# Two-layer streaming encoder on eight cores: lanes half a layer apart from the first weights on, each with its own f32 loads in the first pass

## The chip, the cores and the metric

The kernel runs on all eight cores of one Trainium2 chip. Each core computes one prompt stream and one sample stream; the cores exchange nothing and read the same weights. The metric is the device time of the slowest core, in microseconds.

## What is computed

A network of two layers, for 4096 new frames ("prompt") and 16 frames ("sample") per core, width 1024. Every layer is a mixer and a gated feed-forward block (FFN), each behind an rmsnorm:

```python
for layer in range(DEPTH):            # DEPTH = 2
    # even layer: conv_mixers; odd layer: attention || spatial gating
    x = x + mixer(rmsnorm(x))
    x = x + swiglu(rmsnorm(x, norm_ffn[layer]), w_gate_up[layer], w_down[layer])

def swiglu(h, w_gate_up, w_down):     # FFN_HIDDEN = 2816
    g, up = jnp.split(h @ w_gate_up, 2, axis=-1)
    return (jax.nn.silu(g) * up) @ w_down
```

The even mixer has an input projection of 1024 x 2560, a causal depthwise convolution of width 31 with a layernorm, a convolution of width 3, and an output projection of 1024 x 1024. The odd mixer has an input projection of the same size, attention over the last 576 keys with a relative bias, a spatial gating in blocks of 128 frames, and an output projection. All weights come as f32 and are used as bf16.

## The kernel before

**Tiles and slots.** The prompt's 4096 frames are 8 tiles of 512. All weights of both layers are cut into 96 pieces, called slots (`NPS`, line 458): per layer 10 of the input projection, 4 of the output projection, 22 of gate and up, 12 of down. A slot is 128 x 8 x 256 elements, 512 KB as bf16; 8 of the 12 down slots of a layer have 7 parts instead of 8 (448 KB). For one tile a slot is 16 matmuls of 128x512 (`ws`, line 558), for the sample 16 matmuls of 128x16. Weights don't stay on the core: each tile runs through all 96 slots again. The slots pass through `ring`, nine buffers in SBUF (line 330); buffers 7 and 8 are scratch of the sample until it is done.

**Two lanes and the sample.** Lane A (`lanes[0]`) does tiles 0, 2, 4, 6, lane B (`lanes[1]`) tiles 1, 3, 5, 7, and the sample S goes once through the 96 slots. Each is a generator that yields segments. While the program is built, the loop at lines 1275 to 1325 picks the next segment by a model of time with durations written into it, so the order on every engine is fixed when the program is built. `rank` (lines 1302 to 1311) decides between segments that the model has ready within 0.15 us of each other. Between the lanes, B goes first if A is at least a number of slots ahead, else A: `LAG0` = 3 slots while B is in its first tile, `LAG` = 24 behind it. When the favoured lane isn't ready the other goes.

**Weights in the first pass.** In its first pass a slot is loaded once, from the f32 input `w`, by a DMA on POOL's queue that casts to bf16 (`load_next`, line 465). Both lanes and the sample use that one buffer, which is free again after the third use (`consume`, line 488; the 3 stands in line 493). As lane A comes to a slot, `touch` (line 477) has SP's queue write the bf16 buffer to `wsc` in HBM; the first four slots (`SKIP`) are not written. From each lane's second tile on every lane has buffers and loads of its own, from `wsc`, or from `w` for the first four slots. The DMAs of POOL and of SP each go out in order: a reload that waits holds up all behind it on its queue. A reload waits for TensorE's last use of the buffer and, where the buffer was stored, for that store.

**Other traffic.** x comes in four pieces of 512 KB per tile and y leaves in four, between the down slots of layer 1. The width-31 convolution needs 16 shifted copies of its input per tile (`U<-U`, line 747). The table of attention biases (`Tb`, loaded through `Vb<-rbt`, 1536 KB) is made in the first pass by the prologue, from the flag "late" on, which lane B sets at its fifth gate-up pair (line 644); layer 1 of every lane waits for the flag "Tb" (line 845).

In the views, `L440` is every matmul, `L445` every DMA, `L398` every ScalarE activation, `L411`, `L415` and `L421` VectorE's work; `hT`, `U`, `cat` are a lane's activations, `SM` and parts of `ring` the sample's.

Of the kernel before, what the change touches and what calls it, by code (L numbers as in the profile page):

```python
# [22 lines left out]
LAG = 24  # L23
LAG0 = 3
# [22 lines left out]
class Sched:  # L47
# [176 lines left out]
    def dma(self, eng, fn, sem, rd, wr, us, issue=0.07, load=False):  # L224
# [30 lines left out]
        if load:  # L255
            s = max(start + issue, self.load_free)
            self.load_free = s + us
            b["end"] = max(b["end"], s + us + 2.0)
        else:
            b["end"] = max(b["end"], start + issue + 2.0 + us)  # L260
# [34 lines left out]
def build_program(n_tiles=NPT):  # L295
# [22 lines left out]
    with ExitStack() as es:  # L318
# [146 lines left out]
        def load_next(L):  # L465
            while len(L.loaded) < NPS * L.n_tiles and L.bufs:
                g = len(L.loaded)
                nk = slot_k[g % NPS]
                first = g < NPS or g % NPS < SKIP
                s = L.bufs.pop(0)  # L470
                src = (wv if first else wsv)[g % NPS][:, 0:nk, :]
                dma("pool", ring[:, s, 0:nk, :], src, "ring%d" % s, us=(3.5 if first else 1.8) * nk / 8, load=True)
                L.loaded.append(s)
                if g == NPS - 1:
                    lanes[1].loaded = list(L.loaded)

        def touch(L, sl):
            g = L.th.pos
            if g == len(stored) and g < NPS:
                nk = slot_k[g]  # L480
                if g >= SKIP:
                    dma("sp", wsv[g][:, 0:nk, :], ring[:, sl, 0:nk, :], "st%d" % sl, us=1.8 * nk / 8, load=True)
                stored.append(g)

        def owner(th):
            return lanes[1 if th is thB and th.pos >= NPS else 0]

        def consume(L):
# [4 lines left out]
            if users[O.i, g] == (3 if g < NPS else 1):  # L493
                s = O.loaded[g]
                if s in (4, 5, 6, 8) and len(lanes[0].loaded) >= NPS:
                    O = lanes[1]
                O.bufs.append(s)
# [770 lines left out]
        lanes[0].bufs, lanes[1].bufs = [0, 1, 2], []  # L1268
        load_next(lanes[0])
        first_x(lanes[1], 1, "pool")  # L1270
        lanes[0].bufs.extend([3, 4, 5, 6])
        load_next(lanes[0])
        for th in (thA, thB):
            th.step(None)
        while threads:
            cand = []
            for th in threads:
# [28 lines left out]
                elif th is thS:  # L1306
                    rank = 2 if th.pos <= min(thA.pos, thB.pos + 1) else 4
                elif thA.done or thB.done:
                    rank = 3
                else:  # L1310
                    rank = 3 if (thA.pos - thB.pos >= (LAG0 if thB.pos < NPS else LAG)) == (th is thB) else 5
# [7 lines left out]
            if th is thS and th.done:  # L1319
                lanes[0].bufs.append(7)  # L1320
                load_next(lanes[0])
                O = lanes[1 if len(lanes[0].loaded) >= NPS else 0]
                O.bufs.append(8)
                load_next(O)
# [150 lines left out]
```

How the kernel before makes its waits and increments, by code:

```python
            def emit(handle, eng):  # L1351
                seen = {}
                n = 0
                for fn, waits, sig, inc in S.ops[eng]:
                    for ch, val in waits:
                        v = rank_of[ch][val] if ch in rank_of else S.batches[ch][val]["n"]
                        if seen.get(ch, 0) >= v:
                            continue
                        handle.wait_ge(sems[ch], v)
                        seen[ch] = v
                    ins = fn(handle)
                    if sig in rank_of:
                        n += 1
                        if n in rank_of[sig]:
                            ins.then_inc(sems[sig], 1)
                    elif sig is not None:
                        ins.then_inc(sems[sig], inc)
```

## Time and profile before

| what | us |
|---|---|
| median of 3 runs | 3000.2 (2998.64 to 3558.65) |
| profiled execution, device time | 3000.1 |
| its span, slowest of 8 cores | 2998.5 (the cores lie between 2985.4 and 2998.5) |
| TensorE busy in the span | 2933.1 |

"Busy" is the time in which an engine works on an instruction. The DMA share is the mean busy share of the core's 16 DMA engines, and PEclk is the clock that TensorE was granted, as a part of full speed. A DMA's landing time runs from its issue to its completion and so contains what it queues behind; a queue's share of the 16 engines is what its packets took.

### The profile page before, as it was taken

Reading aid. Unit: us, or ns where it says so; the run is one execution under the profiler, and the core shown is the slowest. Engines: PE = TensorE matmul, PEld = TensorE weight load, DVE = VectorE, ACT = ScalarE, POOL = GpSimd, SP = SyncE. Lnnn points to the kernel's source line nnn. Section 1 sums busy time; section 2 is a strip of 40 time slices with the busy share of each in tenths; the row PEclk is TensorE's granted clock in tenths of the full one; section 3 lists DMA queues with packets and bytes.
Section 4 is the critical chain, followed back from the end, with each engine's and each line's share of the span. In section 5 each row is a group of like instructions: output and inputs, shape, how many; then the busy total and the mean of one; then the engine's idle time right before and its main releaser. Section 6 shows DMA issues by size and latency. Waiting matters only on the chain.

```text
span 2998.5 us, 43471 instructions; the slowest of 8 cores (2985.4 to 2998.5 us)
## 1 busy us (share of the span) xinstructions
PE 2933.1 (98%) x17072; PEld 1388.0 (46%) x17072; DVE 1108.3 (37%) x1452; ACT 1017.2 (34%) x1140; POOL 386.1 (13%) x801
## 2 busy tenths in 40 slices
PE   7999999999999999999999999999999999999999
PEld 3444455444444445444444445444444444544444
DVE  5632144411253224534333333453334242444321
ACT  4421145311133225463232224455223221536410
POOL 1000000000011111111111111111111111111111
PEclk9999999999999999999999999999999999999999
DMA  9766653376983444335566544334665654434434
GB/s 192 159 153 149 140 111 102 85 166 139 217 205 113 149 153 136 118 133 164 167 172 190 174 149 147 127 127 138 172 191 163 178 154 154 134 126 155 141 127 153
DMA packets 125223, 451.83 MB, mean 151 GB/s; under 512 B 17953, under 2 KB 20513, under 8 KB 124898
## 3 DMA queue, kind: packets, MB, share of 16 engines
q0 software_dynamic: 92256, 348.17, 43.4%
q1 hardware_dynamic: 32770, 100.89, 10.8%
q8 instruction: 141, 2.31, 0.3%
q14 instruction: 56, 0.46, 0.1%
HBM read 427.93 MB, written 66.36 MB: 165 GB/s over the span
## 4 chain that ended last, share of the span: by engine, by line
PE 92%; DMA 4%; DVE 2%; ACT 1%; SPq 1%; issue 1%; POOL 0%; DVEq 0%; ACTq 0%; POOLq 0%
PE ps L440 92%; DMA xT<-xp 2%; DMA U<-U 1%; SPq L445 1%; ACT U L398 1%; DVE U L411 0%; DMA ring<-wsc 0%; DVE U L421 0%; ACT hT L398 0%; DVE hT L415 0%; DVE rs L411 0%; ACT cat L398 0%; ACT rs L398 0%; DVE ps L411 0%; ACT L398 0%
## 5 line engine op out<-in xcount | busy, mean ns | idle before, releaser
L440 PE MATMUL ps<-hT,ring 128*128 128x512 bf16 x7680 | 1707.2, 381 | 16.3 <-DVE hT L415 6.4
L440 PEld LDWEIGHTS ps<-hT,ring 128*128 128x128 bf16 x7680 | 743.5, 98 | 928.2 <-issue 63.3
L398 ACT ACTIVATE U<-ps 128x1024 f32<-128x1024 f32 (+3 forms) x448 | 434.0, 981 | 1130.6 <-PE ps L440 924.5
L440 PE MATMUL ps<-U,ring 128*128 128x512 bf16 x3328 | 748.9, 379 | 0.0
L411 DVE TENSOR_TENSOR U<-ps,U 128x1024 bf16<-128x1024 f32 (+2 forms) x240 | 276.4, 1152 | 1012.6 <-PE ps L440 894.8
L440 PEld LDWEIGHTS ps<-U,ring 128*128 128x128 bf16 x3328 | 319.7, 98 | 386.8 <-issue 11.7
L445 POOL DMA_DIRECT2D ring<-wsc x552 | 294.7, 534 | 1568.2 <-PE ps L440 1524.5
L398 ACT ACT_TABLE_LOAD x164 | 210.4, 1283 | 291.1 <-PE ps L440 248.2
L398 ACT ACTIVATE hT<-xT 128x1024 f32<-128x1024 f32 (+1 forms) x118 | 124.1, 1055 | 354.1 <-DVE xT L411 174.6
L411 DVE TENSOR_TENSOR xT<-ps,xT 128x1024 f32<-128x1024 f32 x96 | 117.2, 1223 | 275.8 <-PE ps L440 275.8
L415 DVE SCALAR_TENSOR_TENSOR hT<-rs,vecT,xT 128x512 bf16<-128x512 f32 x256 | 172.3, 746 | 47.3 <-ACT rs L398 44.8
L445 POOL DMA_DIRECT2D ring<-w x120 | 63.7, 533 | 743.5 <-PE ps L440 722.6
L411 DVE TENSOR_TENSOR ps<-ps,Tb 128x768 f32<-128x768 f32 (+1 forms) x144 | 97.8, 695 | 72.7 <-PE ps L440 70.2
L440 PE MATMUL ps<-cat,ring 128*128 128x512 bf16 x512 | 121.0, 379 | 0.7 <-DVE SM L411 0.7
L440 PE MATMUL ps<-ring,hT 128*128 128x256 bf16 x1024 | 119.7, 276 | 1.4 <-ACT cat L398 1.4
L440 PEld LDWEIGHTS ps<-ring,hT 128*128 128x128 bf16 x1024 | 99.8, 99 | 20.2 <-issue 5.6
L411 DVE TENSOR_TENSOR U<-ps,xT 128x1024 f32<-128x1024 f32 x32 | 39.2, 1224 | 141.1 <-PE ps L440 141.1
L421 DVE TENSOR_SCALAR U<-ps,vecT 128x1024 f32<-128x1024 f32 x32 | 41.1, 1284 | 100.2 <-ACT U L398 97.8
L440 PEld LDWEIGHTS ps<-cat,ring 128*128 128x128 bf16 x512 | 49.2, 98 | 59.2 <-issue 1.5
L440 PE MATMUL ps<-U,ones 128*64 128x512 bf16 (+1 forms) x480 | 64.0, 303 | 4.7 <-ACT U L398 4.6
L440 PE MATMUL ps<-U,convW 128*32 128x512 bf16 x1024 | 58.5, 387 | 6.1 <-DMA U<-U 5.9
L440 PE MATMUL ps<-U,Vb 128*64 128x512 bf16 (+1 forms) x480 | 62.8, 299 | 0.0
(141 smaller groups left out, 1097.2 us busy)
## 6 DMA issues: line engine op xcount, KB each, us to landing
ring<-wsc POOLq DMA_DIRECT2D x456, 512.0 KB, 3.7
ring<-w POOLq DMA_DIRECT2D x104, 512.0 KB, 7.2
ring<-wsc POOLq DMA_DIRECT2D x96, 448.0 KB, 3.6
wsc<-ring SPq DMA_DIRECT2D x76, 512.0 KB, 5.0
U<-U SPq DMA_DIRECT2D x128, 134.5 KB, 8.0
yp<-U SPq DMA_DIRECT2D x32, 512.0 KB, 5.9
xT<-xp SPq DMA_DIRECT2D x22, 512.0 KB, 8.1
ring<-w POOLq DMA_DIRECT2D x16, 448.0 KB, 5.8
```

Source lines behind the costliest of these rows:

```text
L398: return e.activation(out=out, in_=in_, func=func, **kw)
L411: return S.add("dve", lambda e: e.tensor_tensor(out=out, in0=in0, in1=in1, op=op), [in0, in1], [out], dcost(in0))
L415: return S.add("dve", lambda e: e.scalar_tensor_tensor(out=out, in0=in0, scalar=scalar, in1=in1, op0=op0, op1=op1), rd, [out], dcost(in0, 1))
L421: return e.tensor_scalar(out=out, in0=in0, scalar1=s1, scalar2=None, op0=op0)
L440: return S.add("pe", lambda e: e.matmul(out, lhsT, rhs, start=start, stop=stop), [lhsT, rhs], [out], c)
L445: return S.dma(eng, lambda e: e.dma_start(out=out, in_=in_), sem, [in_], [out], us, issue, load)
```

## The change

Each lane now has its own buffers and loads from the first slot on: A (with the sample) buffers 0 to 3, B buffers 4 to 6; after the sample A gets 7 and B gets 8. In the first pass each lane loads every slot from f32. A buffer of lane A is free after two uses in the first pass (A and S), one of B after one. The lag of 3 holds only until B has done two slots; from then on it is 30 slots, where a layer has 48. The bf16 copies are written while lane A is in its second pass, whose loads are therefore from f32 too; lane B's second pass and all later ones load copies. All 96 slots are now stored. The costs in the model of time change as well: an f32 load counts 3.4 us instead of 3.5, and a store occupies the modelled DMA without waiting for earlier loads.

In the program this makes 288 loads from `w` (240 of 512 KB, 48 of 448 KB) where there were 120 (104 and 16), 480 loads from `wsc` (400 and 80) where there were 552 (456 and 96), and 96 stores where there were 92.

```diff
--- before.py
+++ after.py
@@ -20,7 +20,7 @@
 NEG = -30000.0
 SLOT = 4096
 KB = 12
-LAG = 24
+LAG = 30
 LAG0 = 3
 JIT = 4
 SKIP = 4
@@ -252,7 +252,10 @@
                 snap[a] = v
         b["snap"] = snap
         self.t[eng] = start + issue
-        if load:
+        if load == "store":
+            self.load_free = max(start + issue, self.load_free) + us
+            b["end"] = max(b["end"], start + issue + 2.0 + 2 * us)
+        elif load:
             s = max(start + issue, self.load_free)
             self.load_free = s + us
             b["end"] = max(b["end"], s + us + 2.0)
@@ -465,36 +468,31 @@
         def load_next(L):
             while len(L.loaded) < NPS * L.n_tiles and L.bufs:
                 g = len(L.loaded)
-                nk = slot_k[g % NPS]
-                first = g < NPS or g % NPS < SKIP
+                n = g % NPS
+                nk = slot_k[n]
+                first = g < NPS or n >= len(stored)
                 s = L.bufs.pop(0)
-                src = (wv if first else wsv)[g % NPS][:, 0:nk, :]
-                dma("pool", ring[:, s, 0:nk, :], src, "ring%d" % s, us=(3.5 if first else 1.8) * nk / 8, load=True)
+                dma("pool", ring[:, s, 0:nk, :], (wv if first else wsv)[n][:, 0:nk, :], "ring%d" % s, us=(3.4 if first else 1.8) * nk / 8,
+                    load=True)
                 L.loaded.append(s)
-                if g == NPS - 1:
-                    lanes[1].loaded = list(L.loaded)
 
         def touch(L, sl):
             g = L.th.pos
-            if g == len(stored) and g < NPS:
-                nk = slot_k[g]
-                if g >= SKIP:
-                    dma("sp", wsv[g][:, 0:nk, :], ring[:, sl, 0:nk, :], "st%d" % sl, us=1.8 * nk / 8, load=True)
+            if L.i == 0 and NPS <= g < 2 * NPS and g - NPS == len(stored):
+                nk = slot_k[g - NPS]
+                dma("sp", wsv[g - NPS][:, 0:nk, :], ring[:, sl, 0:nk, :], "st%d" % sl, us=1.8 * nk / 8, load="store")
                 stored.append(g)
 
         def owner(th):
-            return lanes[1 if th is thB and th.pos >= NPS else 0]
+            return lanes[1 if th is thB else 0]
 
         def consume(L):
             g = L.th.pos
             O = owner(L.th)
             L.th.pos += 1
             users[O.i, g] = users.get((O.i, g), 0) + 1
-            if users[O.i, g] == (3 if g < NPS else 1):
-                s = O.loaded[g]
-                if s in (4, 5, 6, 8) and len(lanes[0].loaded) >= NPS:
-                    O = lanes[1]
-                O.bufs.append(s)
+            if users[O.i, g] == (2 if O.i == 0 and g < NPS else 1):
+                O.bufs.append(O.loaded[g])
                 load_next(O)
 
         flags = set()
@@ -1265,11 +1263,10 @@
         dma("sp", smp.cst, sst[:, :], "sst", us=4)
         thP.step(None)
         S.add("pool", lambda e: e.memset(tailA[:, 0, 0:1], 0.0), [lanes[0].xT[:, 0:2, :]], [tailA[:, 0, 0:1]], 0.1)
-        lanes[0].bufs, lanes[1].bufs = [0, 1, 2], []
+        lanes[0].bufs, lanes[1].bufs = [0, 1, 2, 3], [4, 5, 6]
         load_next(lanes[0])
         first_x(lanes[1], 1, "pool")
-        lanes[0].bufs.extend([3, 4, 5, 6])
-        load_next(lanes[0])
+        load_next(lanes[1])
         for th in (thA, thB):
             th.step(None)
         while threads:
@@ -1304,11 +1301,11 @@
                 elif not seg.slot:
                     rank = 1
                 elif th is thS:
-                    rank = 2 if th.pos <= min(thA.pos, thB.pos + 1) else 4
+                    rank = 2 if th.pos <= thA.pos else 4
                 elif thA.done or thB.done:
                     rank = 3
                 else:
-                    rank = 3 if (thA.pos - thB.pos >= (LAG0 if thB.pos < NPS else LAG)) == (th is thB) else 5
+                    rank = 3 if (thA.pos - thB.pos >= (LAG0 if thB.pos < 2 else LAG)) == (th is thB) else 5
                 cand.append((t, rank, th, b))
             t0 = min(c[0] for c in cand)
             t, rank, th, b = min((c for c in cand if c[0] <= t0 + 0.15), key=lambda c: c[1])
@@ -1317,11 +1314,9 @@
                 pairs_free.remove(b)
             th.step((b, owner(th).loaded[th.pos] if seg.slot else None))
             if th is thS and th.done:
-                lanes[0].bufs.append(7)
-                load_next(lanes[0])
-                O = lanes[1 if len(lanes[0].loaded) >= NPS else 0]
-                O.bufs.append(8)
-                load_next(O)
+                for i in range(2):
+                    lanes[i].bufs.append(7 + i)
+                    load_next(lanes[i])
             threads[:] = [x for x in threads if not x.done]
 
         fin = []
```

**TensorE in the first FFN of the first tiles.** In the rows `hT0` is lane A's input, `hT1` lane B's, `SM` the sample's; x16 is one slot of a lane. Before:

```order
L440 MATMUL ps<-hT1,ring 128x512 x16
L440 MATMUL ps<-SM,ring 128x16 x16
L440 MATMUL ps<-hT0,ring 128x512 x16
L440 MATMUL ps<-hT1,ring 128x512 x16
L440 MATMUL ps<-SM,ring 128x16 x16
```

Changed, from lane B's eighth slot and the slots 14 to 17 of lane A on:

```order
L443 MATMUL ps<-hT1,ring 128x512 x16
L443 MATMUL ps<-SM,ring 128x16 x32
L443 MATMUL ps<-hT0,ring 128x512 x32
L443 MATMUL ps<-SM,ring 128x16 x16
L443 MATMUL ps<-hT0,ring 128x512 x16
L443 MATMUL ps<-SM,ring 128x16 x16
L443 MATMUL ps<-hT0,ring 128x512 x16
```

Before, lane A and lane B take turns slot by slot. Changed, after lane B's eighth slot (first row) lane A and the sample go on alone, up to lane A's slot 37.

**TensorE ahead of lane A's first attention layer, changed.** `rs0` and `hT0` with `o1024` are lane A's norm, `kT 128x512` belongs to the making of the bias table, and the last row is lane A's slot 48:

```order
L443 MATMUL ps<-hT1,ring 128x512 x32
L443 MATMUL ps<-rs0,o1024 128x512 x2
L443 MATMUL ps<-hT0,o1024 128x512 x2
L443 MATMUL ps<-hT1,ring 128x512 x48
L443 MATMUL ps<-kT 128x512 x2
L443 MATMUL ps<-hT1,ring 128x512 x96
L443 MATMUL ps<-SM,ring 128x16 x16
L443 MATMUL ps<-hT0,ring 128x512 x16
```

Eleven slots of lane B (18 to 28) stand in a row here (x32, x48 and x96), with four more (14 to 17) a little ahead of them. Lane A is 30 slots ahead when they begin and 19 when its layer 1 does.

**TensorE from lane A's second tile on.** `convW` is the convolution of width 31. Before, from lane A's first slots to the convolution of lane B:

```order
L440 MATMUL ps<-hT0,ring 128x512 x32
L440 MATMUL ps<-rs1,o1024 128x512 x2
L440 MATMUL ps<-hT1,o1024 128x512 x2
L440 MATMUL ps<-hT0,ring 128x512 x128
L440 MATMUL ps<-hT1,ring 128x512 x16
L440 MATMUL ps<-U0,convW 32x512 x128
L440 MATMUL ps<-hT1,ring 128x512 x48
L440 MATMUL ps<-U0,o512 128x512 x2
L440 MATMUL ps<-rs0,o512 128x512 x2
L440 MATMUL ps<-hT1,ring 128x512 x96
L440 MATMUL ps<-cat0,ring 128x512 x8
L440 MATMUL ps<-U0,ring 128x512 x8
L440 MATMUL ps<-U1,convW 32x512 x128
```

Changed, lane A's first slots and what follows them:

```order
L443 MATMUL ps<-hT0,ring 128x512 x32
L443 MATMUL ps<-hT1,ring 128x512 x64
L443 MATMUL ps<-hT0,ring 128x512 x16
L443 MATMUL ps<-hT1,ring 128x512 x48
L443 MATMUL ps<-U0,convW 32x512 x128
L443 MATMUL ps<-hT1,ring 128x512 x48
L443 MATMUL ps<-U0,o512 128x512 x2
L443 MATMUL ps<-rs0,o512 128x512 x2
L443 MATMUL ps<-hT0,ring 128x512 x16
L443 MATMUL ps<-hT1,ring 128x512 x16
```

Before, both lanes do their ten input slots together, and the two convolutions stand 9 slots apart. Changed, lane A's convolution stands among lane B's output projection and gate and up slots of layer 1 (x64, x48, x48).

**SP's queue, where the stores stand.** Before, from the start of the program:

```order
L445 DMA ring<-sst 128x252
L445 DMA U0<-U0 32x2152 x16
L445 DMA wsc<-ring 128x2048 x2
L445 DMA U1<-U1 32x2152 x16
L445 DMA wsc<-ring 128x2048 x4
L445 DMA cas<-ring 512x1x30
L445 DMA cbs<-ring 512x1x2
L445 DMA wsc<-ring 128x2048 x14
```

Changed, from the end of lane A's first tile on:

```order
L448 DMA xT0<-xp 128x1024
L448 DMA yp<-U0 128x1024
L448 DMA xT0<-xp 128x1024
L448 DMA ys<-SM 128x128
L448 DMA yp<-U0 128x1024
L448 DMA wsc<-ring 128x2048 x4
L448 DMA U0<-U0 32x2152 x16
L448 DMA wsc<-ring 128x2048 x13
L448 DMA hT1<-xp 128x1024
L448 DMA wsc<-ring 128x2048 x3
L448 DMA yp<-U1 128x1024
```

The stores moved from the first weights on to behind the first tile's last y piece, where lane A's replicas and lane B's x and y pieces go out as well.

## Rows read from the trace of the kernel before

**Rows 1.** The page: busy us of each engine (part 1), POOL's DMA queue (part 3)

```profile
PE 2933.1 (98%) x17072; PEld 1388.0 (46%) x17072; DVE 1108.3 (37%) x1452; ACT 1017.2 (34%) x1140; POOL 386.1 (13%) x801
...
q0 software_dynamic: 92256, 348.17, 43.4%
```

**Rows 2.** Windows: engines' busy us by stretch, then granted clock, DMA share, GB/s

```profile
0.00:150.00 150.00, 128.08 (x1018) 60.86 (x1019) 86.45 (x168) 67.50 (x102) 13.14 (x30) 0.98 0.83 176
150.00:375.00 225.00, 225.00 (x1409) 107.20 (x1408) 58.93 (x78) 38.84 (x49) 17.44 (x35) 1.00 0.66 148
375.00:600.00 225.00, 215.87 (x1708) 116.08 (x1707) 99.12 (x159) 106.44 (x151) 15.25 (x38) 0.98 0.46 99
600.00:750.00 150.00, 150.00 (x947) 71.86 (x946) 25.46 (x29) 21.05 (x27) 11.62 (x22) 1.00 0.71 153
750.00:975.00 225.00, 210.63 (x1252) 94.87 (x1251) 88.90 (x119) 60.33 (x70) 25.37 (x48) 0.97 0.72 179
975.00:2998.50 2023.50, 2003.54 (x10745) 937.17 (x10742) 749.42 (x899) 723.06 (x742) 303.25 (x628) 1.00 0.49 152
```

**Rows 3.** Timeline of TensorE, 17 to 70: start, us, line, operands, count

```profile
17.63 1.09 PE L440 MATMUL ps<-SM,ring 128*128 128x16 bf16 x16 [2.15 <-DMA ring<-w]
...
44.80 0.55 PE L440 MATMUL ps<-SM,ring 128*128 128x16 bf16 x16
...
45.41 17.43 PE L440 MATMUL ps<-hT,ring 128*128 128x512 bf16 x80
62.87 7.10 PE L440 MATMUL ps<-U,convW 128*32 128x512 bf16 x128
```

**Rows 4.** DMA, 150 to 375: queues (packets, MB, share), issues (count, KB, landing)

```profile
q0 software_dynamic: 4392, 15.44, 45.2%
q1 hardware_dynamic: 4898, 17.57, 20.7%
...
wsc<-ring SPq DMA_DIRECT2D x23, 512.0 KB, 3.8
ring<-w POOLq DMA_DIRECT2D x23, 512.0 KB, 7.0
ring<-w POOLq DMA_DIRECT2D x8, 448.0 KB, 5.4
wsc<-ring SPq DMA_DIRECT2D x8, 448.0 KB, 2.5
```

**Rows 5.** DMA, 30 to 40, with no other queue at work

```profile
q0 software_dynamic: 479, 1.75, 102.5%
```

**Rows 6.** DMA, 1000 to 1100

```profile
q0 software_dynamic: 3729, 14.90, 45.5%
...
ring<-wsc POOLq DMA_DIRECT2D x22, 512.0 KB, 3.5
ring<-wsc POOLq DMA_DIRECT2D x8, 448.0 KB, 3.3
```

**Rows 7.** DMA, 40 to 150

```profile
q1 hardware_dynamic: 4608, 11.82, 41.7%
...
wsc<-ring SPq DMA_DIRECT2D x14, 512.0 KB, 10.1
...
U<-U SPq DMA_DIRECT2D x32, 134.5 KB, 6.8
```

**Rows 8.** DMA, 750 to 850

```profile
q0 software_dynamic: 2809, 10.01, 58.0%
q1 hardware_dynamic: 3656, 12.04, 41.1%
...
ring<-w POOLq DMA_DIRECT2D x9, 512.0 KB, 11.7
...
wsc<-ring SPq DMA_DIRECT2D x2, 512.0 KB, 20.9
```

**Rows 9.** Waits of POOL: us in total, times, longest

```profile
POOL ring L445 <- DMA wsc<-ring: 23.0, 3, 10.7
```

## The prediction

> **What bounds the kernel now.** I read the page's busy line first, then busy time by stretch, then who is waited for, then the DMA queues. TensorE is busy 2933.1 of 2998.5 us [rows 1]; all that a change of order can touch is the 65.4 us in which it idles, plus what a lowered clock costs. The stretches say where they lie [rows 2]: 21.9 us in the first 150, none in 150 to 375, 9.1 in 375 to 600 (both lanes at attention together), none in 600 to 750, 14.4 in 750 to 975 (the lanes are pulled apart from 3 slots to 24 while all 16 DMA engines are full), 20.0 in the 2023.5 us of steady state and tail behind it. The clock column reads 0.98, 0.98 and 0.97 in the three stretches with stalls and 1.00 elsewhere: about 0.02 x 128 + 0.02 x 216 + 0.03 x 211 = 13 us. So faster by 2% (60 us, about what a measurement of this kernel can tell from no change) would need nearly all of the idle time and clock loss at once.
>
> The other resource is DMA. In the first pass a slot's weights are loaded once for both lanes and the sample, so a load is wanted about every 7 us and the DMA share is only 0.66 [rows 2]. Prices per full slot (512 KB as bf16): TensorE needs (62.87 - 45.41) / 5 = 3.49 us for a lane's 16 matmuls and 0.41 us (45.21 - 44.80) for the sample's [rows 3]. For DMA I divide a queue's share by its transfers. 150 to 375: 45.2% of 225 us = 101.7 us over 23 + 8 x 0.875 = 30 loads from f32 = 3.4 us of all 16 engines each, with a store beside each; on SP's queue 20.7% of 225 = 46.6 us, less 4.8 for a table of 1536 KB, over 30 stores: 1.4 to 1.45 us [rows 4]. Alone on the engines such loads are cheaper: in 30 to 40 us POOL's queue moved 1.75 MB, 3.34 slots, in 102.5% of 10 us: 3.07, say 3.0 to 3.1 us [rows 5]. The bf16 copies in steady state: 45.5 us over 29 loads = 1.57 us [rows 6]. Conv replicas: SP's queue spent 41.7% of 110 = 45.9 us in 40 to 150; less 14 stores at 1.45, 25.6 us for 32 issues, so 0.80 each, 12.8 us for a tile's 16 [rows 7]. An x or y transfer moves the bytes of a copy's load, 512 KB: 1.6 us.
>
> **The change, part by part.** Traffic: weights are loaded from f32 288 times instead of 120 and from the bf16 copies 480 times instead of 552; stores are 96 instead of 92. In full slots: 164 more at 3.4, 70 fewer at 1.57, 4 more at 1.45: 558 - 110 + 6 = 454 us of DMA, so POOL's queue, 43.4% now [rows 1], should read about 58%, or down to 56% as far as loads without stores beside them are cheaper. Whether that costs time is a question of stretches. I walk the new order by slots (A, B the lanes, S the sample; "A14" is lane A's 15th weight slot) and set TensorE's need against DMA's, first at the dearer 3.4 us.
>
> A0-13 with B0-7: TensorE 22 x 3.49 + 14 x 0.41 + 14.2 for one lane's conv (2 x 7.10 [rows 3]) + 2 = 99 us; DMA 22 x 3.4 + 12.8 + 6.4 for the second x = 94. A14-37 with S alone: 94 against 82. A38-47 with B8-28: 123 against 120 (a conv, a set of replicas and the table in it). A48-61, B29-34 and the sample's attention: about 100 against 71. A62-95 with B35-57: 221 against 195. In each of these DMA keeps up, and without stores, at 3.1 us, it has a tenth to spare. The stretch that does not fit is A96-129 with B58-95. Lane A now loads its second pass from f32 too, and the stores fall there. TensorE: 71 full slots x 3.49 + 14.2 + 6 = 268 us. DMA: 67 loads from f32 (34 for A, 33 for B), four bf16 loads 6, 34 stores x 1.45 = 49, ten x and y transfers 16, replicas 13. A store stands beside every second load, so I price these between the two rows, at 3.2: 214, in all 298 us, short by 30. Slack of earlier stretches is lost, because only nine buffers can hold loads ahead; full at the start and nearly empty at the end they give back about six loads, 19 us. So I take **+10 us** there. Bounds: 0 at 3.1 us, where the shortage of 22 about fits the buffers (and in 750 to 850 the two queues took 58.0 + 41.1 = 99% of the engines [rows 8], inside a stretch that idles 14.4 us in all); +43 at 3.4 with no help from the buffers, +23 with it. Behind it a pair of slots needs 3.4 + 1.45 + 1.57 = 6.4 us of DMA against 6.98, so the backlog melts by 0.6 us a pair while lane B's replicas come: **+3** (0 to +12).
>
> The start: the first load still lands at about 17 us [rows 3], but four loads of lane A now stand ahead of lane B's x and three of B's behind it, and A4's load, issued when A0 is done near 24 us, stands behind all of it (7 loads x 3.1 + 6.4 = 28 us from 9 us on, then its own 3.1: about 40). TensorE has A0-3 and B0-1 until about 46. Chosen **0** (bounds -6, if one conv at a time stalls less; +12, if the 99 and 94 above are served in the wrong order). The middle of the pass: attention of one lane beside the other's FFN; but the flag that starts the bias table is set by lane B at its 23rd slot, and lane A's layer 1 waits for the table. So B runs B14-17 and B18-28 almost alone on three buffers: a cycle of 3.49 for use, some 0.5 for issue and the 7.0 us in which a load lands beside a store [rows 4] is 11.0, against 3 x 3.49 = 10.5: 0.2 us per slot at most, some 3 us in all, and less with no store beside it. Against the 9.1 us that idle there now I take **-5** (-9 to +3). The pulling apart at 750 to 975 goes: **-14.4** (-14.4 to -5). In steady state a lag of 30 instead of 24 moves the lanes' norms against each other, but neither places two of them together; the 24 loads of the first four slots that were always f32 become copies. **0** (-4 to +4): 20.0 us over three rounds of both lanes and the tail is little to win. Stores on SP's queue wait for their loads there and stand ahead of y, x and replicas; what these lose I count in the +3. Clock: **0** (-8 to +3).
>
> Sum: 0 - 5 - 14.4 + 10 + 3 + 0 = -6.4. The profiled execution took 3000.1 us (span 2998.5, 1.6 around it), the median of the runs is 3000.2; 3000.1 - 6.4 is 2993.7, **2994**.
>
> The load's price decides the sign. Beside stores the trace has 3.4 us, alone 3.07 [rows 4, 5]; a load reads 1.05 MB, so alone it runs at 342 GB/s. The Trainium skill (DMA: Bandwidth & Descriptors, Specifications) gives about 358 GB/s as a core's HBM limit, which the trace without stores comes near to. Taken as the limit beside stores too, the page gives an estimated 2.9 us a load, 20 us less in that stretch, and a shortage that the buffers hold: the result is then that of the first rival. The trace's 3.4 speaks against it, and my sum goes by the rows.
>
> **Rivals.** (1) The buffers swallow the overload: f32 loads cost 3.1 us among stores too, the order takes whichever slot is ready, and y and x fall outside. Then 0 at the overload and behind it, -9 in the middle, -14.4 for the pulling apart, and half of the clock's 13 us back: -30, **2970 us**. For it: the 99% of DMA in 750 to 850. Against it: that lasted 100 us with the ring full ahead of it; this lasts 270. (2) Slower by over 2%: POOL's queue blocks. A slot of lane A cannot be reloaded before its own store has read it, POOL issues in order for both lanes, and behind a waiting reload stands B's. Stores took 20.9 us to land under full DMA, f32 loads 11.7 [rows 8]: 33 us, and five buffers of A at a pair's 7 us give 35. It decides from the point at which the two together pass 35 us. The wait has been there three times, up to 10.7 us [rows 9]. At 2 us for each of 34 reloads it costs 68 on top of the forecast: **3062 us**. Against it: a store goes out as soon as its load is in, before TensorE comes to the slot. (3) The mixed price holds: 3.4 us and 23 at the overload, 5 behind it, 0 in the middle because lane B has caught up before A48: 0 + 0 - 14.4 + 23 + 5 = +14, **3014 us**. (4) The change doesn't do what it says: the lag of 30 is in place by A38, but B is at 19 when A48 starts, so the lanes meet norm and attention as now, and the f32 loads hide; the pulling apart is then only moved: **3000 us**.
>
> **Chances.** Forecast 0.40, rival 1 0.27, rival 2 0.07, rival 3 0.19, rival 4 0.07. The range, 2960 to 3040, takes in rivals 1, 3 and 4 with some spread around them and the bounds of the terms as far as they don't all come together (+12, +43 and +12 with nothing won would), and leaves out rival 2. Faster by over 2%: 0.02; within 2%: 0.91; slower: 0.07 (rival 2).
>
> **What would show it.** After: POOL's queue at 56 to 58%; DMA share 0.8 to 0.9 through most of the first 600 us and about 1.0 for 250 us from some 650 us on; in that stretch TensorE waits for ring loads from f32, 5 to 20 us in all, and they land in over 10 us; stalls of under 5 us between 300 and 600. Wrong would be: waits for f32 loads of under 3 us in all (rival 1), POOL's waits for stores of more than 50 us (rival 2), waits of over 20 us for f32 loads (rival 3), DMA at 0.95 before the stores begin (then 3.1 us is wrong), or a steady state that changed by more than 5 us.

## The result: slower by 1.0%, and the profile after

The changed kernel takes 1.010 times the time of the kernel before (95% interval 1.0075 to 1.0125): 3025.83 and 3031.64 us against 2998.64 to 3001.16. (The median over all four runs, 3252, mixes in two in which cores ran at a lower clock, as happens to the kernel before too; the ratio leaves these out.) The forecast of 2994 had the wrong sign. The time lies inside the stated range, nearest to rival 3 (3014).

The page's first line and POOL's DMA queue of the changed kernel, answering to [rows 1]:

```profile
PE 2918.5 (97%) x16782; PEld 1385.3 (46%) x17072; DVE 1109.7 (37%) x1452; ACT 1066.4 (35%) x1175; POOL 436.9 (14%) x897
...
q0 software_dynamic: 107104, 397.46, 57.6%
```

The traffic is as forecast: POOL's queue at 57.6%, where 58% stood for 3.4 us a load and 56% for cheaper ones. TensorE's busy time did grow: 290 matmul records are missing on cores 2 and 4 (core 4 is the one shown) and 298 on the same two cores of the kernel before, and on the six cores with full traces the mean busy time rose from 2928.4 to 2936.5 us. Busy time by stretch on the slowest core, columns as in [rows 2]:

```profile
0.00:150.00 150.00, 115.58 (x870) 52.80 (x882) 74.37 (x152) 58.37 (x90) 17.92 (x39) 0.92 0.81 156
150.00:375.00 225.00, 219.11 (x1527) 108.86 (x1552) 76.16 (x114) 59.97 (x80) 33.85 (x65) 1.00 0.91 145
375.00:600.00 225.00, 218.73 (x1602) 113.88 (x1625) 72.80 (x112) 78.15 (x109) 28.01 (x53) 0.98 0.78 126
600.00:750.00 150.00, 142.11 (x1003) 70.75 (x1019) 51.12 (x71) 58.87 (x65) 21.20 (x50) 0.99 0.89 161
750.00:975.00 225.00, 204.51 (x995) 89.77 (x1013) 60.29 (x64) 42.55 (x47) 27.50 (x52) 0.98 1.02 200
975.00:3021.00 2046.00, 2018.45 (x10794) 949.21 (x10983) 774.96 (x940) 768.50 (x786) 308.47 (x638) 1.00 0.59 171
```

Against [rows 2] there are three differences. The first 150 us idle 34.4 us instead of 21.9 and the granted clock reads 0.92 instead of 0.98. The stretch 750 to 975, which should have lost its 14.4 us, idles 20.5, with DMA at 1.02. And the last row idles 27.6 of 2046 us, where [rows 2] idle 20.0 of 2023.5; but 189 of the missing records fall into it, and the core of [rows 2] lacks none. DMA reads 1.01 to 1.04 from 700 to 1100 us, so this row also mixes the end of the overload with the steady state. (At 1300 to 1400 it reads 1.02 once more, and TensorE idles only 0.7 us.) I therefore cut the time at 650, 1100 and 1400 us below, and take the mean over all eight cores of the idle time (stretch less TensorE's busy time) and of the granted clock:

| us idle, mean of 8 cores | 0-150 | 150-650 | 650-1100 | 1100-1400 | 1400-2980 |
|---|---|---|---|---|---|
| before | 22.8 (clock 0.982) | 10.9 | 13.2 | 2.7 | 12.0 |
| changed | 33.9 (0.924) | 9.7 | 26.3 | 0.5 | 6.4 |

Differences: +11.1, -1.2, +13.1, -2.2, -5.6 of idle time, and the clock: (0.982 - 0.924) x about 117 us busy = 7 in the start and 2 in the third stretch. Together +24 us. The mean span of the eight cores rose from 2990.3 to 3013.9, by 23.5, so this table holds the change. The six full traces alone give +13.1 of idle time (+11.1 in the start and +11.1 at 650 to 1100, where they idle 24.1 us) and +8.1 of busy time, for a mean span longer by 21.2.

The metric is the slowest core, and the cores came apart: 2985.4 to 2998.5 us before, 2999.8 to 3024.3 now. The two ends of the changed kernel:

```profile
core 3: 2999.8 us, clock 0.994
core 4: 3024.3 us, clock 0.991
```

Core 3 idles 18.8 us at 650 to 1100, core 4 35.9 (its trace lacks records; core 7, with a full one, idles 31.9).

Who is waited for at 650 to 1100 in the changed kernel (slowest core; us in total, times, longest):

```profile
PE ps L443 <- DMA ring<-w: 22.1, 11, 4.0
PE ps L443 <- DMA U<-U: 4.9, 1, 4.9
PE ps L443 <- DVE hT L418: 2.7, 2, 2.2
```

and POOL's queue in the same stretch:

```profile
POOL ring L448 <- DMA wsc<-ring: 154.7, 18, 25.9
```

The loads from f32 end most of TensorE's idle time there. It had another cause before. Core 7 at 650 to 1100, before and changed, full traces:

```profile
PE ps L440 <- DVE hT L415: 6.2, 2, 3.9
```

```profile
PE ps L443 <- DMA ring<-w: 23.1, 13, 4.9
...
PE ps L443 <- DVE hT L418: 2.7, 2, 2.2
```

On the mean of the six full traces TensorE waits there for VectorE and ScalarE (the norms) 8.7 us before and 2.7 changed, and for DMA 4.1 before and 20.5 changed.

POOL's queue stood 154.7 us behind stores in this stretch, against 23.0 us in the whole kernel before [rows 9]. Both rival 2 (the queue blocks) and rival 3 (too many us of DMA) fit these rows; two experiments below tell them apart. DMA in the worst 250 us, columns as in [rows 8]:

```profile
q0 software_dynamic: 8798, 31.00, 73.0%
q1 hardware_dynamic: 6623, 23.04, 27.4%
...
ring<-w POOLq DMA_DIRECT2D x28, 512.0 KB, 17.8
...
ring<-w POOLq DMA_DIRECT2D x16, 448.0 KB, 15.4
```

Together 100.4% of the 16 engines, and a load from f32 takes 15.4 to 17.8 us to land, where [rows 4] have 7.0.

### The profile page after: what moved, and what is told of

It reads as the page before. It is cut to its first block, busy times and chain, and to the rows that moved or that the text cites. A ratio compares the mean times of both kernels' runs of the same rounds, so it can differ in the third digit from the quotient of the medians.

```text
span 3024.3 us, 43480 instructions; the slowest of 8 cores (2999.8 to 3024.3 us)
## 1 busy us (share of the span) xinstructions
PE 2918.5 (97%) x16782; PEld 1385.3 (46%) x17072; DVE 1109.7 (37%) x1452; ACT 1066.4 (35%) x1175; POOL 436.9 (14%) x897
## 3 DMA queue, kind: packets, MB, share of 16 engines
q0 software_dynamic: 107104, 397.46, 57.6%
## 4 chain that ended last, share of the span: by engine, by line
PE 86%; DMA 8%; issue 2%; DVE 1%; SPq 1%; ACT 1%; POOL 0%; DVEq 0%; ACTq 0%; POOLq 0%
PE ps L443 86%; DMA ring<-w 4%; DMA wsc<-ring 2%; SPq L448 1%; DMA U<-U 1%; DMA ring<-wsc 1%; DVE hT L418 0%; ACT U L401 0%; DVE U L414 0%; DMA xT<-xp 0%; ACT L401 0%; DVE U L424 0%; ACT cat L401 0%; ACT rs L401 0%; POOL ring L448 0%
## 5 line engine op out<-in xcount | busy, mean ns | idle before, releaser
L443 PE MATMUL ps<-hT,ring 128*128 128x512 bf16 x7506 | 1693.2, 380 | 39.4 <-DMA ring<-w 13.1
L401 ACT ACTIVATE U<-ps 128x1024 bf16<-128x1024 f32 (+2 forms) x448 | 435.1, 981 | 1075.4 <-PE ps L443 896.0
L443 PE MATMUL ps<-U,ring 128*128 128x512 bf16 x3249 | 744.4, 380 | 14.5 <-DMA ring<-w 7.6
L448 POOL DMA_DIRECT2D ring<-wsc x480 | 256.6, 535 | 1294.9 <-PE ps L443 1263.7
L448 POOL DMA_DIRECT2D ring<-w x288 | 152.7, 532 | 1030.4 <-PE ps L443 821.0
L443 PE MATMUL ps<-U,convW 128*32 128x512 bf16 x1024 | 65.1, 418 | 15.0 <-DMA U<-U 15.0
L401 ACT ACTIVATE U<-ps,vecT 128x512 f32<-128x512 f32 (+1 forms) x48 | 31.2, 685 | 92.1 <-PE ps L443 92.0
```

The source lines that it names most:

```text
L401: return e.activation(out=out, in_=in_, func=func, **kw)
L443: return S.add("pe", lambda e: e.matmul(out, lhsT, rhs, start=start, stop=stop), [lhsT, rhs], [out], c)
L448: return S.dma(eng, lambda e: e.dma_start(out=out, in_=in_), sem, [in_], [out], us, issue, load)
```

## The experiments

Times are ratios to the kernel before on the same chip; "start", "first pass" and "second pass" are the stretches 0-150, 150-650 and 650-1100, with the mean idle time of eight cores as in the table.

**Own loads without the stagger.** The changed kernel with the lanes 3 slots apart through the first tile.

```diff
-... (LAG0 if thB.pos < 2 else LAG)) ...
+... (LAG0 if thB.pos < NPS else LAG)) ...
```

> The changed kernel, own f32 loads for each lane, but lane B held 3 slots behind lane A through the whole first tile, as before. If the extra traffic alone costs the time, it stays at 3025 or above, near 3035, as both lanes' convolutions and attention fall together and the lanes are pulled apart while stores and f32 loads run. If it is the stagger in the start that costs (the convolution waits for its replicas with little else to do), the first 150 us idle 22 us or less again and the time is 3010 to 3020.

Measured: 1.0185 (1.016 to 1.0211), some 3058 us. Idle 33.3, 17.5 and 34.0 us. The slowest core:

```profile
0.00:150.00 150.00, 114.06 (x837) 52.00 (x849) 73.15 (x146) 54.80 (x83) 18.00 (x39) 0.91 0.89 164
150.00:650.00 500.00, 480.60 (x3358) 245.30 (x3412) 176.17 (x264) 162.74 (x222) 67.07 (x138) 0.99 0.81 124
650.00:1100.00 450.00, 405.46 (x2304) 184.12 (x2345) 132.13 (x165) 93.08 (x107) 57.67 (x109) 0.95 0.97 192
```

So the change is two parts of opposite sign: own loads (and the stores in lane A's second pass with them) at the old lag cost some 56 us, and pulling the lanes apart from the start gives back some 26 of them. The start idles as long at a lag of 3 as in the changed kernel (33.3 against 33.9), so the second guess of the expectation falls: without the stagger it is no shorter. It is not made of the same waits, though. On the six full traces 8.4 us of it are waits for DMA and 24.8 others, where the changed kernel has 15.5 and 17.9 and the kernel before 4.6 and 17.6.

**Only the lag.** The kernel before with `LAG = 30`.

```diff
-LAG = 24
+LAG = 30
```

> The kernel before with LAG = 30 instead of 24 and nothing else. If the lag in steady state costs nothing (my term of 0), the time is 3000 within 4. If the lag of 30 brings norms of the two lanes together and is part of the loss, 3006 to 3015.

Measured: 0.9995 (0.9978 to 1.0012). The lag of 30 in steady state costs nothing.

**Stores in the first pass.** `touch` writes the copies while lane A is in its first tile:

```diff
-            if L.i == 0 and NPS <= g < 2 * NPS and g - NPS == len(stored):
+            if L.i == 0 and g < NPS and g == len(stored):
```

> The changed kernel, but the bf16 copies are written in lane A's first pass, so lane A's second pass loads copies. If the loss comes from the second pass (reloads held by stores beside loads from f32, some 650 to 1100 us), the waits of POOL for stores there (154.7 us in 18 in the changed kernel) move to the first pass or go, and TensorE's waits for f32 loads at 850 to 1100 (22.1 us) go; the time falls from about 3028 to 3005 to 3012, unless the same waits come up in the first pass. Rival, the start: the first 150 us hold the loss (34 us idle there against 22, and a clock of 0.92 against 0.98), this edit does not touch it or makes it worse, and the time stays at 3025 to 3035.

Measured: 1.0181 (1.015 to 1.0212), some 3057 us where at most 3012 was expected, and slower than the changed kernel, not faster. The second pass is healed, 12.4 us, and the loss has moved: 38.8 in the start and 34.2 in the first pass, with DMA at 1.00 there instead of 0.82. The total of DMA work is less than in the changed kernel (q0 and q1 62.4% against 68.1%), but it now stands where both lanes load from f32.

**A part of the stores in the first pass.** Slots 14 to 35 and 48 to 61 are stored in lane A's first pass, where my walk saw room, the others in its second.

```diff
-                first = g < NPS or n >= len(stored)
+                first = g < NPS or n not in stored
...
+            n = g % NPS
+            if L.i == 0 and g < 2 * NPS and n not in stored and (g >= NPS or 14 <= n < 36 or 48 <= n < 62):
```

> The changed kernel with 36 of the 96 copies (slots 14 to 35 and 48 to 61) written in lane A's first pass, where the DMA had some room, and the rest in its second; lane A's second pass loads copies for the 36. If the overload of the second pass (too many us of DMA between 850 and 1100) costs time by itself, it loses 36 x (3.4 - 1.6) + 36 x 1.45 = 117 us of DMA there, the waits for loads from f32 at 650 to 1100 (22.1 us) fall under 8, and the time is 3010 to 3018, if the first pass pays under 5. If the stores in the first pass cost what they spare, as they did when all stood there (3058), 3028 to 3040.

Measured: 3040.3 and 3047.1 us, too few for an interval. The two stretches on the slowest core:

```profile
150.00:650.00 500.00, 477.40 (x3376) 238.31 (x3375) 158.89 (x239) 154.91 (x206) 64.97 (x126) 0.97 0.93 166
650.00:1100.00 450.00, 440.25 (x2495) 202.93 (x2492) 150.85 (x187) 122.68 (x137) 64.99 (x131) 0.99 0.90 192
```

The second pass falls to 11.0 us of idle (mean) and the first rises from 9.7 to 25.2: what is spared in the one comes up in the other (and from 1400 us on it idles 16.6 instead of 6.4). So 36 stores (52 us of DMA) don't fit into a first pass whose DMA share reads 0.82; my walk had 12 and 29 us of room in just those places.

**Stores that no reload waits for.** Each store reads a constant tile; the copies then don't hold the weights.

```diff
-dma("sp", wsv[g - NPS][:, 0:nk, :], ring[:, sl, 0:nk, :], ...)
+dma("sp", wsv[g - NPS][:, 0:nk, :], convW[:, 0:8 * nk, :] (reshaped), ...)
```

> The changed kernel with every store reading a constant tile instead of the ring buffer, so the same bytes go out but no reload waits for a store, and SP's queue waits for no load; left out is that the copies hold the weights, so all passes behind the second of lane A compute with other numbers. If the loss at 650 to 1100 us comes from reloads held behind stores on POOL's queue (my rival 2, priced at 68 us, POOL's wait 154.7 us there), POOL's wait for stores falls to 0, TensorE's waits for loads from 22.1 to under 8 us, and the time to 3010 to 3016. If the traffic by itself is too much, the waits stay at 15 us or more and the time within 5 us of 3028.

Measured: 1.0151 (1.0128 to 1.0174). TensorE's and POOL's waits at 650 to 1100 on the slowest core:

```profile
PE ps L443 <- DMA ring<-w: 16.4, 11, 3.9
```

```profile
POOL ring L448 <- DMA wsc<-convW: 6.2, 2, 3.5
```

POOL's waits for stores are gone, 154.7 to 6.2 us, and the stretch idles 25.0 us on the mean core where the changed kernel idles 26.3, with DMA at 1.02. Rival 2 is refuted as a cause: the queue stood behind stores, but without these waits the 16 engines were as full and TensorE idled as long. The kernel as a whole is 15 us slower than the changed one, which neither theory said: in the first pass TensorE waits once for ScalarE for up to 11 and 15 us on two of the cores, and the steady stretches idle 7 us more each. The order differs from the second pass on, the first pass should not; what makes these waits I can't say.

**A second pass that is light on DMA.** Lane A's second pass loads the first stored copy in place of its own f32 slot; its second tile is computed with wrong weights.

```diff
+                light = L.i == 0 and NPS <= g < 2 * NPS and len(stored) > 0
+                first = first and not light
...
-(wv if first else wsv)[n][:, 0:nk, :]
+(wv if first else wsv)[0 if light else n][:, 0:nk, :]
```

> The changed kernel, but from the moment that one copy is stored lane A's second pass loads that first copy (1.6 us of DMA) in place of its own slot from f32 (3.4 us); stores, their waits and everything else stay. Left out is that lane A's second tile is computed, and stored, with its own weights. If the overload of DMA makes the idle time at 650 to 1100 us (26 us on the mean of the cores, 13 to 14 in the kernel before), some 30 loads less by 1.8 us are 54 us of DMA, more than the shortage of 43: idle there 8 to 13 us, and the time 3008 to 3016. If it is another thing of that stretch, as stores ahead of reloads or the order, it stays over 20 us and the time at 3025 or more.

Measured: 1.0054 (1.0029 to 1.0079). Core 4, whose stretch reads 35.9 in the changed kernel, and POOL's wait on the slowest core:

```profile
650.00:1100.00 450.00, 435.58 (x2382) 197.94 (x2424) 159.49 (x199) 123.33 (x137) 64.89 (x130) 0.99 0.89 223
```

```profile
POOL ring L448 <- DMA wsc<-ring: 88.1, 16, 18.4
```

Idle falls to 13.1 us (mean), 14.4 on core 4, with DMA at 0.89 instead of 1.01, although POOL still waits 88 us for stores. On the six full traces TensorE's waits for DMA there fall from 20.5 to 7.5 us. With the experiment before it this settles the second pass: the overload of the DMA engines costs 13 us of the mean core and some 21 of core 4, the waits for stores next to nothing. (From 1400 us on this kernel idles 14.5 us where the changed one idles 6.4; the order of its matmuls differs there, and that loss is not explained.)

**No copies at all.** Every load from f32, no stores.

```diff
-                first = g < NPS or n >= len(stored)
+                first = True
```

> The changed kernel with no copies at all: every load from f32, no stores. It tells the price of f32 loads without stores. At 3.0 to 3.1 us a load against 3.49 us of TensorE a slot, DMA keeps up apart from x, y and replicas: the stretch from 650 to 1100 us loses its 36 us of idle down to some 10, POOL waits for no store, and the later passes pay a little: 3005 to 3030, DMA share about 0.95 throughout. If f32 loads cost 3.4 us without stores too, TensorE falls behind everywhere and the time is over 3080.

Measured: 1.0121 (1.0096 to 1.0147), some 3038 us. POOL's queue:

```profile
q0 software_dynamic: 112224, 397.46, 80.8%
```

80.8% of 3037.8 us less 13 for x and caches is some 2442 us over 640 + 128 x 0.875 = 752 full loads: 3.25 us each with no store anywhere. The second pass idles 13.0 us; steady state 24.7 instead of 6.4, at a DMA share of 0.89. So steady state lost about 1%, but not by late weights: on the six full traces 7.1 us of the waits from 1400 us on are for replicas and 0.6 for loads from f32, while waits for ScalarE rise from 3.0 to 11.3. The order of the segments changed too, so how much of the 1% is DMA's stays open.

**Three tries at the start.** Lane B 3 slots behind until it has done 14:

```diff
-... (LAG0 if thB.pos < 2 else LAG)) ...
+... (LAG0 if thB.pos < 14 else LAG)) ...
```

> The changed kernel, but lane B stays 3 slots behind lane A until it has done 14 slots of its first tile instead of 2. If the start loses because lane A's convolution has too little beside it, the first 150 us idle 22 to 28 us instead of 34 and the time falls by 5 to 10 us, to some 3020. If the start is bound by the loads themselves (own loads held 3 apart idled 36 us there as well), nothing is won: 3025 to 3035.

Measured: 1.0149 (1.0133 to 1.0165); start 35.2 us. Lane B's x and loads only after lane A's tenth slot:

```diff
+            if late_b and thA.pos >= 10:
+                late_b = False
+                first_x(lanes[1], 1, "pool")
+                load_next(lanes[1])
+                thB.step(None)
+                threads.append(thB)
```

> The changed kernel, but lane B's first x and its first loads go out only when lane A has done 10 slots. The convolution's wait for its replicas (6.0 and 4.2 us in the first 150) is then short if it was lane B's loads that the replicas queued behind; the first 150 us would idle under 28 us. Against it, lane B can fill nothing in the first 60 us. Theory of the queue: 3015 to 3025. Theory that the start lacks other work: idle of 38 us or more in the first 150 and 3030 to 3040.

Measured: 1.0126 (1.0103 to 1.0149); start 32.4 us. The replicas of the first tiles counted as 14 us in the model of time:

```diff
-us=REPUS if t > 1 else 4.0
+us=REPUS if t > 1 else 14.0
```

> The changed kernel with one number of the model of time changed: the replicas of the first two tiles count 14 us instead of 4, so that the order puts more slots ahead of these convolutions. In the changed kernel DMA is busy only 0.42 of 50 to 100 us while TensorE waits 6.0 us for the replicas and, in order behind the convolution, releases no buffer. If it is this place in the order that costs, the first 150 us idle 26 to 29 us instead of 34 (median of the cores) and the time falls by 5 to 8 us, to some 3022. If the start is bound by the f32 loads of both lanes, the wait only turns into one for ring loads, 34 us idle and 3026 to 3032.

Measured: 1.0113 (1.0097 to 1.0129); start 32.9 us. Its TensorE:

```profile
59.21 10.52 PE L443 MATMUL ps<-hT,ring 128*128 128x512 bf16 x48
69.66 7.10 PE L443 MATMUL ps<-U,convW 128*32 128x512 bf16 x128
...
101.59 0.58 PE L443 MATMUL ps<-SM,ring 128*128 128x16 bf16 x16 [3.50 <-DMA ring<-w]
...
125.69 8.56 PE L443 MATMUL ps<-hT,ring 128*128 128x512 bf16 x32 [8.48 <-DMA ring<-w]
```

The convolution no longer waits (69.66 starts without a wait, against 5.98 us of idle before 63.78 below), but 3.5 and 8.5 us of waits for loads stand behind it, and DMA is busy 0.94 of the start. All three moved the waits; none took more than 1.5 us from them. And all three idle 31.2 to 32.7 us at 650 to 1100, 5 us or more above the changed kernel, though none of the edits aims at that stretch: a few us of difference there are not to be read as an effect.

**The steady state's gain, alone.** The kernel before with `SKIP = 0`, and the same with `LAG = 30` too.

```diff
-SKIP = 4
+SKIP = 0
```

> The kernel before with all 96 slots stored and loaded as copies from the second pass on (SKIP = 0), so 24 loads from f32 less. From 1100 us on the changed kernel idles 3.5 us on a core with a full trace, the kernel before some 9 to 14, and the kernel before with a lag of 30 about 8. If the f32 loads of the first four slots make up the rest, this kernel idles 5 to 9 us there and runs at 2995 to 2999 beside 3001. If they are nothing, 3001.

> The kernel before with SKIP = 0 and LAG = 30 together: the steady state of the changed kernel behind the first pass of the kernel before. Idle from 1100 us on 3 to 5 us as in the changed kernel; the pulling apart to 30 slots costs what it costs at 24 or some us more (17 against 14). 2993 to 2998.

Measured: 0.9964 (0.9949 to 0.9979) and 0.9966 (0.9952 to 0.9979), some 11 us faster than the kernel before, more than expected. The mean core gained 6 us; the rest is that the cores lie closer together (5 to 12 us apart, where the kernel before has 13 to 22 beside them). Core 5 of the first, the stretches from 650 us on:

```profile
650.00:1100.00 450.00, 441.06 (x2539) 202.65 (x2537) 138.94 (x171) 97.48 (x112) 52.45 (x99) 0.99 0.62 167
1100.00:1400.00 300.00, 297.88 (x1731) 144.53 (x1729) 128.09 (x162) 153.77 (x155) 46.77 (x108) 1.00 0.42 135
1400.00:2980.00 1580.00, 1573.94 (x8432) 733.33 (x8431) 587.90 (x706) 547.77 (x566) 236.88 (x484) 1.00 0.50 156
```

and the same core of the changed kernel:

```profile
650.00:1100.00 450.00, 423.61 (x2271) 188.19 (x2269) 147.01 (x176) 116.42 (x128) 60.95 (x121) 0.98 1.02 211
1100.00:1400.00 300.00, 300.00 (x1695) 145.68 (x1692) 115.42 (x136) 155.74 (x152) 46.28 (x103) 1.00 0.82 200
1400.00:2980.00 1580.00, 1576.51 (x8490) 733.88 (x8489) 602.25 (x733) 573.40 (x591) 239.05 (x492) 1.00 0.52 159
```

From 1400 us on the idle time of this core is 6.1 us (13.1 before, 3.5 in the changed kernel), and 8.9 against 14.4 at 650 to 1100, where the first four slots of both lanes used to be loaded from f32; on the six full traces the waits for DMA fall there from 4.1 to 1.0 us, and the waits for the norms stay (8.7 and 8.5). These two kernels beat both the one before and the changed one.

## Why the prediction was wrong

The forecast was the sum 0 - 5 - 14.4 + 10 + 3 + 0 = -6; on the mean core it came out as +11 - 1 + 13 (for the three terms -14.4 + 10 + 3 together) - 8 + 9 = +24. Two steps failed, by some 15 and 18 us: the second pass, forecast at -1.4 and measured at +13, and the start, forecast at 0 and measured at +11 with 7 us of clock on top.

**The second pass: -1.4 forecast, +13 measured.** I walked the order rightly to the stretch that does not fit (A96-129 with B58-95), and then priced its 67 loads from f32 at 3.2 us, between 3.4 [rows 4] and 3.07 [rows 5]. The first pass of the changed kernel holds hardly any stores, so it tests the price without them:

```profile
q0 software_dynamic: 18827, 64.47, 81.5%
...
ring<-w POOLq DMA_DIRECT2D x102, 512.0 KB, 6.6
ring<-w POOLq DMA_DIRECT2D x21, 448.0 KB, 6.6
Vb<-cv POOLq DMA_DIRECT2D x1, 512.0 KB, 10.9
kT<-ck POOLq DMA_DIRECT2D x1, 512.0 KB, 12.9
```

The last two also come from f32 and land as bf16, so 81.5% of 500 us is 407.5 us over 102 + 21 x 0.875 + 2 = 122.4 loads: 3.33 us (3.2 to 3.4 on the eight cores), nearly alone on the engines; without any store in the whole kernel it was 3.25. In the second pass itself, 650 to 1100 us on the same core:

```profile
q0 software_dynamic: 15537, 55.27, 74.6%
...
ring<-w POOLq DMA_DIRECT2D x73, 512.0 KB, 12.0
...
ring<-wsc POOLq DMA_DIRECT2D x18, 512.0 KB, 17.1
```

74.6% of 450 us less 18 copies at 1.57 is 307 us. The queue moved 55.27 MB; less 9.44 for the copies, that is 87.4 full loads: 3.5 us each, and 3.4 to 3.5 on the eight cores. The load was mis-sized by some 0.25 us, 17 us over 67 loads. The 3.07 was one window of 10 us at the start, with a pile of loads queued one behind the other; why loads were cheaper there is not shown.

At 3.4 us I had written +23 and +5 (rival 3), with the pulling apart gone (-14.4): the stretch would idle 13 - 14.4 + 28 = 27 us. It idles 26.3, but that it agrees so well is partly luck. By the waits (six full traces) the overload and what follows it cost 20.5 us of waits for DMA, more than the 13 of the forecast and less than the 28 of rival 3. And pulling the lanes apart took waits for the norms from 8.7 to 2.7 us, not to nothing. I had read the 14.4 us of [rows 2] as the price of pulling apart under full DMA; on the mean two thirds of the waits in that stretch were for the norms. The lighter second pass, at 13.1, shows that the f32 traffic makes the difference between 13 and 26.

**The start: 0 forecast, +11 measured**, at the upper bound I gave (+12), and 7 us of clock on top of it, which stand in the clock's term below. I compared sums, 99 us of TensorE with 94 of DMA, and took that as fitting. But they have to fit in order. In the changed kernel's start:

```profile
17.84 1.09 PE L443 MATMUL ps<-SM,ring 128*128 128x16 bf16 x16 [1.69 <-DMA ring<-w]
...
45.11 8.83 PE L443 MATMUL ps<-hT,ring 128*128 128x512 bf16 x31 [3.90 <-DVE hT L418]
...
54.19 3.61 PE L443 MATMUL ps<-hT,ring 128*128 128x512 bf16 x16
63.78 9.76 PE L443 MATMUL ps<-U,convW 128*32 128x512 bf16 x128 [5.98 <-DMA U<-U]
...
111.73 0.71 PE L443 MATMUL ps<-SM,ring 128*128 128x16 bf16 x16 [3.32 <-DMA ring<-w]
...
128.12 10.01 PE L443 MATMUL ps<-U,convW 128*32 128x512 bf16 x128 [4.15 <-DMA U<-U]
```

Lane B's first slots wait for its norm (45.11), slot 4 follows, and then the convolution stands 5.98 us for its replicas with the queue of TensorE blocked behind it; at 111.73 a ring load is late and at 128.12 lane B's replicas. The 128 matmuls of the convolution take 9.76 and 10.01 us here and 7.10 in [rows 3]: behind these two waits the granted clock reads 0.50, half of full speed, from 64 to 68 and from 128 to 134 us, where [rows 3] have 1.00. On the six full traces the waits for replicas rise from 2.9 us in the kernel before to 10.8 and those for loads from 1.8 to 4.7, and all others stay (17.6 and 17.9): that is the +11.

Where the 94 us of DMA work went can be seen too. The engines are full up to 64 us and again from 100 to 130 us (1.02), but from 66 to 100 us they read 0.15 (0.13 to 0.21 on the eight cores). POOL's queue in these us:

```profile
78.24 0.53 POOL L448 DMA_DIRECT2D ring<-w  x1 [19.37 <-PE ps L443]
96.37 0.53 POOL L448 DMA_DIRECT2D ring<-w  x1 [17.60 <-PE ps L443]
99.83 2.65 POOL L448 DMA_DIRECT2D ring<-w  x5 [2.93 <-PE ps L443]
```

One reload waits 17.60 us for TensorE to release its buffer; soon after it five go out in a row without a wait, so their buffers had come free in the meantime. The sum had room, but the queue's fixed order could not use it. The three tries show that neither the lag, nor lane B's traffic, nor the place of the convolution is the cause by itself: with the order mended (the replicas' time at 14) this gap is filled in good part (0.82 from 66 to 100 us on the mean core), DMA reads 0.94 over the start, and the wait becomes one for loads. That each lane's own loads are the cause, and not the stagger, rests on the lag of 3 with own loads, 33.3 us; as that kernel's start is made of other waits, this is likely and not shown.

**The middle: -5 forecast, -1 measured.** Nothing was won: attention of one lane beside the other's FFN idles about as much as both together; on the six full traces waits for ScalarE and VectorE fell from 8.5 to 6.1 us, and waits for loads rose from 0.9 to 2.3. Lane B's run of 15 slots on three buffers did no harm: the waits for f32 loads are 4.1 us in this pass on the slowest core.

**Steady state: 0 forecast, -8 measured.** I gave ±4, and named a change of over 5 us as a sign of being wrong. The idle time at 1100 to 2980 us on the mean core is 14.7 before, 12.6 with the lag of 30, 12.1 with `SKIP = 0`, 10.6 with both, 6.9 in the changed kernel. So the lag and the 24 loads give some 2 us each, and nearly half of the 8 belongs to neither; what gave it is open. TensorE's waits for DMA there were 0.5 us before, so it is waits for ScalarE (10.0 before, 3.0 changed) that went.

**The clock: 0 forecast, +9 measured**; it is lower in the stretches that idle more. The busy time of the six full traces, longer by 8.1 us, says the same.

Rival 1 (the buffers swallow the overload, 2970) was wrong with the price on which it stood. Measured loads read 1.05 MB in 3.2 to 3.4 us without stores and 3.4 to 3.5 us beside them, which is 312 to 327 and 298 to 309 GB/s. The Trainium skill (DMA: Bandwidth & Descriptors, Specifications) gives about 358 GB/s as a core's HBM limit, from which I had estimated 2.9 us a load; these loads don't reach it. Rival 2's wait for stores came, 154.7 us of it, and cost nothing that the overload did not cost anyway.

## What to carry to other kernels

Price a transfer from the stretch that looks most like its new place, not from the window with the best rate; where two rows disagree by a tenth and the sum hangs on it, take the one whose traffic looks like that of the new place. A DMA share of 0.82 over a pass is not room: 36 stores put into it cost as much as they saved elsewhere. Nor does a sum of DMA time below TensorE's say that the two fit: in the start the engines stood at 0.15 for 34 us, because one reload waited at the head of the queue, and were full on both sides of it. And a wait that is long and new is not yet a cause: POOL stood 155 us behind stores, and taking that wait away changed the stretch by 1 us, while lightening the traffic beside it brought the stretch back to the idle time it had before. Last, look at what a stretch waits for before you book its idle time as a gain: 14.4 us were booked as the price of pulling the lanes apart, and part of the norm waits among them stayed.

## What was not expected of the hardware

A load from f32 that lands as 512 KB of bf16 took 3.07 us of the 16 engines in one window, 3.2 to 3.4 in a pass without stores and 3.4 to 3.5 beside stores. And a DMA share of 1.0 has no fixed price: on core 4 TensorE idled 32 us in the 400 us from 700 on, at shares of 1.01 to 1.04, and 0.7 us in the 100 us from 1300 on, at 1.02.

The cores of the changed kernel lie 24.5 and 24.8 us apart (in the runs of 3025.83 and 3031.64 us), which looks like the work of full DMA engines; but the kernel before lies 11.6 to 30.0 us apart in the runs that the experiments are compared with (18 on the mean), so that is not shown. What is shown is the other direction: with 24 loads of f32, 3.6% of its 672 weight loads, turned into copies (and four stores more), the kernel before is 11 us faster on its slowest core, 6 of them on the mean core and the rest because its cores lie only 6 to 8 us apart.
